# VectorE and ScalarE operations of a two-block decoder kernel wait for the last operation on their engine that they depend on, set call by call, instead of always for the one issued just ahead

## The reference

```python
for l in range(2):                      # first block
    h = rms_norm(x, norm_w[l]);  p = h @ w_in[l]
    qa, ka, va, za, ub, zb, qkv_c, b_c, a_c, zc = _split_cols(p)
    oa = sliding_window_sink_attention(rope(rms_norm(qa)), rope(rms_norm(ka)), va, sinks[l]) * silu(za)
    ob = conformer_conv_module(ub, ...) * silu(zb)      # 31 taps, layer norm, silu, a 512x512 map
    oc = rms_norm(gated_deltanet(qkv_c, b_c, a_c, ...)) * silu(zc)   # 4 taps, chunks of 128 tokens
    x = x + concatenate([oa, ob, oc]) @ w_out[l]
for i in range(2):                      # second block
    u, z = split(rmsnorm(x, g_pre[i]) @ w_in_2[i])
    y = pool_mixer(u) if i == 0 else rglru(causal_depthwise_conv_2(u))
    x = x + rmsnorm((y * silu(z)) @ w_out_2[i], g_post[i])
    gate = sigmoid(rmsnorm(x, g_ple_in[i]) @ w_ple_gate[i])
    x = x + rmsnorm((p[i] @ w_ple[i]) * gate, g_ple_out[i])
```

## Time and profile before

| | |
|---|---|
| median of 3 runs | 2496.28 us (2494.63 to 2497.04) |
| the profiled execution, its own time | 2496.72 us |
| its span in the profile | 2494.9 us |
| PE busy | 2429.7 us (97%), 14580 matmuls |
| PE loading weights | 2144.0 us (86%) |
| DVE busy | 1729.0 us (69%), 1895 instructions |
| ACT busy | 1281.8 us (51%), 1378 instructions |
| granted TensorE clock, mean | 0.993 |

### The profile page before, as it was taken

How to read it: one execution, slowest core, us unless ns; L and a number is a source line. 1 busy time by engine, 2 the same in 40 slices (tenths; PEclk the granted TensorE clock), 3 DMA queues, 4 the chain that set the end, 5 groups by cost and what they waited for, 6 DMA issues and landing times.

```text
span 2494.9 us, 34361 instructions
## 1 busy us (share of the span) xinstructions
PE 2429.7 (97%) x14580; PEld 2144.0 (86%) x14580; DVE 1729.0 (69%) x1895; ACT 1281.8 (51%) x1378; POOL 0.2 (0%) x4
## 2 busy tenths in 40 slices
PE   8999999999999999999999999999999999999997
PEld 8998888799988987888888888878888888888876
DVE  5789757666898567566657667666657757678774
ACT  5544345654452365644444434356656466566573
POOL 0000000000000000000000000000000000000000
PEclk9999999999999999999999999999999999999999
DMA  6553223455532234555555555555454545555553
GB/s 230 203 182 123 94 92 123 179 223 187 186 136 95 102 117 161 206 186 186 186 190 190 194 186 186 194 209 192 152 182 176 191 178 186 187 185 186 197 191 118
DMA packets 63978, 428.19 MB, mean 172 GB/s; under 512 B 7120, under 2 KB 7248, under 8 KB 14800
## 3 DMA queue, kind: packets, MB, share of 16 engines
q1 hardware_dynamic: 61280, 414.97, 46.2%
q10 hardware_dynamic: 2544, 11.01, 1.2%
HBM read 421.76 MB, written 4.19 MB: 171 GB/s over the span
## 4 chain that ended last, share of the span: by engine, by line
PE 71%; DVE 16%; ACT 7%; issue 5%; DMA 0%; DVEq 0%; ACTq 0%; SPq 0%
PE PS L419 69%; DVE WL L1643 4%; DVE Q L1608 3%; DVE Q L1612 3%; ACT Q L971 3%; DVE QA L1612 2%; ACT WH L985 2%; ACT QA L971 1%; PE PS L542 1%; DVE O L1608 1%; PE PS L647 1%; DVE QA L2207 0%; DVE QA L1608 0%; DVE X L1612 0%; DVE Q L1619 0%
## 5 line engine op out<-in xcount | busy, mean ns | idle before, releaser
L1643 DVE TENSOR_TENSOR WL<-W,WH 128x2048 fp32r<-128x2048 f32 (+2 forms) x392 | 859.6, 2202 | 456.1 <-ACT WH L985 455.4
L985 ACT ACTIVATE WH<-W 128x2048 fp32r<-128x2048 f32 (+2 forms) x392 | 716.0, 1839 | 459.5 <-PE PS L419 363.9
L419 PE MATMUL PS<-H,WH 128*128 128x256 f32 (+1 forms) x4864 | 947.5, 328 | 0.0
L419 PEld LDWEIGHTS PS<-H,WH 128*128 128x128 f32 x4864 | 714.0, 191 | 44.0
L419 PE MATMUL PS<-H,WL 128*128 128x256 f32 x3392 | 561.1, 285 | 12.3 <-DVE H L1612 9.1
L419 PEld LDWEIGHTS PS<-H,WL 128*128 128x128 f32 x3392 | 503.9, 191 | 59.0 <-issue 12.7
L419 PE MATMUL PS<-WH,H 128*128 128x512 f32 (+1 forms) x1408 | 366.6, 381 | 0.0
L419 PEld LDWEIGHTS PS<-WH,H 128*128 128x128 f32 x1408 | 259.0, 188 | 51.6
L419 PE MATMUL PS<-WH,YS 128*128 128x512 f32 x1024 | 273.8, 389 | 0.0
L419 PEld LDWEIGHTS PS<-WH,YS 128*128 128x128 f32 x1024 | 192.2, 188 | 40.1
L419 PE MATMUL PS<-WL,H 128*128 128x512 f32 (+1 forms) x704 | 217.0, 388 | 8.5 <-DVE H L1608 8.5
(11 more groups left out here) (140 smaller groups left out, 1572.7 us busy)
## 6 DMA issues: line engine op xcount, KB each, us to landing
W<-in_wall SPq DMA_DIRECT2D x374, 1024.0 KB, 4.8
W<-in_wall SPq DMA_DIRECT2D x24, 512.0 KB, 3.5
W<-in_wall SPq DMA_DIRECT2D x8, 536.0 KB, 3.5
X<-in_xT SPq DMA_DIRECT2D x8, 256.0 KB, 5.8
X<-in_x ACTq DMA_DIRECT2D x1, 2048.0 KB, 8.7
xsave<-X ACTq DMA_DIRECT2D x1, 2048.0 KB, 8.6
X<-xsave ACTq DMA_DIRECT2D x1, 2048.0 KB, 7.9
Q<-in_g_post ACTq DMA_DIRECT2D x8, 256.0 KB, 3.3
```

The costliest lines, as they stand in the source:

```text
L419: return e.matmul(o, l, r, start=start, stop=stop, skip_group_check=True)
L985: e.activation(WH[:, s % NSPL, 0:m], W[:, c % NRAW, 0:m], ACT.Copy).then_inc(*up("hi", c))
L1643: e.tensor_tensor(WL[:, c % NRAW, 0:m], W[:, c % NRAW, 0:m], WH[:, s % NSPL, 0:m].bitcast(F32), ALU.subtract).then_inc(*up("lo", c))
```

## The change

Both lists of the last signals are kept whole (`past`), and each call says with `lag` how many of the operations issued just ahead it need not wait for: lag 0 is the wait as before, lag 3 waits for the fourth last. By a count of the calls, 951 of DVE's 1503 such operations and 342 of ACT's 800 have a lag above 0. Two places are also written in another order. The core of the diff:

```diff
             def act(o, a, f, *sig, lag=0, **k):
-                if here["end"]:
-                    w.wait_ge(*here["end"])
+                if len(past) > lag:
+                    w.wait_ge(*past[-1 - lag])
                 sig = sig or ("step_a",)
                 e.activation(o, a, f, **k).then_inc(*up(*sig))
-                here["end"] = (K.sem[sig[0]], K.count[sig[0]])
+                past.append((K.sem[sig[0]], K.count[sig[0]]))
...
                     act(rn[:, 512 * k:512 * k + 512], sbank("dn", l, "ss", k), ACT.Ln, "dn_a", l, "ln", k,
-                        scale=1.0, bias=tb("eps"))
+                        scale=1.0, bias=tb("eps"), lag=min(k, 3))
...
-                    act(TT_[:, 512 * k:512 * k + 512], sbank("dn", l, "tu", k), ACT.Copy, "dn_a", l, "tu", k)
+                    act(TT_[:, 512 * k:512 * k + 512], sbank("dn", l, "tu", k), ACT.Copy, "dn_a", l, "tu", k,
+                        lag=k)
...
                             act(p3[:, h, c0:c1], s3[:, h, c0:c1], ACT.Exp, bias=sm[:, 56 + k:57 + k], scale=1.0,
-                                accum_out=sm[:, 80 + k:81 + k])
+                                accum_out=sm[:, 80 + k:81 + k], lag=min(2 * (h - 4 * q) + b_, 3))
...
-            def before():
-                if here["end"]:
-                    w.wait_ge(*here["end"])
+            def before(lag=0):
+                if len(past) > lag:
+                    w.wait_ge(*past[-1 - lag])
...
             def summed(dst, g):
                 w.wait_ge(*to("ev_a", g))
                 for b in range(2):
-                    tt(dst(b), dst(b), sums(g, b, 1), ALU.add)
-                    tt(dst(b), dst(b), rb(2), ALU.mult, *(("ev_v", g) if b else ()))
+                    tt(dst(b), dst(b), sums(g, b, 1), ALU.add, lag=b)
+                for b in range(2):
+                    tt(dst(b), dst(b), rb(2), ALU.mult, *(("ev_v", g) if b else ()), lag=1)
...
                         stt(CT[:, 4 * i + m, :], RAW[:, 4 * i + m, k:k + 256], wk, CT[:, 4 * i + m, :], ALU.mult,
-                            ALU.add, *end)
+                            ALU.add, *end, lag=n - 1 if k else m)
...
-                    tt(KB[:, cs], CK[:, cs], sbank("dn", l, "bt", k), ALU.mult, "dn_v", l, "kb", k)
+                    tt(KB[:, cs], CK[:, cs], sbank("dn", l, "bt", k), ALU.mult, "dn_v", l, "kb", k, lag=k)
...
                     tt(DS[:, cs], sbank("dn", l, "kk", k), DS[:, cs], ALU.mult, "dn_v", l, "kk", k)
-                    tt(quad(UU[:, cs]), quad(DS[:, cs]), tbl("lv2").unsqueeze(1).to_broadcast([128, 4, 128]), ALU.mult)
+                    w.wait_ge(*to("dn_p", l, "kq", k))
+                    tt(DI[:, cs], sbank("dn", l, "kq", k), DI[:, cs], ALU.mult, "dn_v", l, "kq", k, lag=1)
+                    tt(quad(UU[:, cs]), quad(DS[:, cs]), tbl("lv2").unsqueeze(1).to_broadcast([128, 4, 128]), ALU.mult,
+                       lag=1)
                     tt(quad(UU[:, cs]), quad(UU[:, cs]), ident.unsqueeze(1).to_broadcast([128, 4, 128]), ALU.add,
                        "dn_v", l, "uu", k)
-                    w.wait_ge(*to("dn_p", l, "kq", k))
-                    tt(DI[:, cs], sbank("dn", l, "kq", k), DI[:, cs], ALU.mult, "dn_v", l, "kq", k)
...
-                        stt(ACC[:, m, :], HB[:, m, k:k + 256], wk, ACC[:, m, :], ALU.mult, ALU.add, *end)
+                        stt(ACC[:, m, :], HB[:, m, k:k + 256], wk, ACC[:, m, :], ALU.mult, ALU.add, *end,
+                            lag=3 if k else m)
...
                         stt(s3[:, h, :], sbank("at", l, "s", h)[:, 0:384], 0.125, tbl("amask", 384), ALU.mult, ALU.add,
-                            "at_v", l, "s", h)
+                            "at_v", l, "s", h, lag=h % 4)
...
                         stt(X[:, t, cs], E[:, t, cs], SM[:, 12 + t:13 + t], X[:, t, cs], ALU.mult, ALU.add,
-                            *(("x_v", "end", l, i) if t else ()))
+                            *(("x_v", "end", l, i) if t else ()), lag=min(2 * i + t, 3))
```

More of the change, by code:

```diff
@@ L1021, in first_sums @@
                 for b in range(2):
-                    act(dst(b), sums(g, b, 0), ACT.Copy, *(("ev_a", g) if b else ()))
+                    act(dst(b), sums(g, b, 0), ACT.Copy, *(("ev_a", g) if b else ()), lag=b)
             def skip(n):
@@ L1113, in decays @@
                     act(heads(EG)[:, 2 * k:2 * k + 2, 1, :], quad(sbank("dn", l, "eg", k))[:, 1::2, :], ACT.Exp,
-                        "dn_a", l, "eg", k, scale=1.0, bias=0.0)
-                    act(DI[:, cs], DI[:, cs], ACT.Exp, "dn_a", l, "di", k, scale=1.0, bias=0.0)
+                        "dn_a", l, "eg", k, scale=1.0, bias=0.0, lag=2 if k else 0)
+                    act(DI[:, cs], DI[:, cs], ACT.Exp, "dn_a", l, "di", k, scale=1.0, bias=0.0, lag=1)
             def delta_net(l):
@@ L1212, in attention @@
                     w.wait_ge(*to("at_p", l, "qt", k))
-                    act(dst, sbank("at", l, "qt", k), ACT.Copy, "at_a", l, "qt", k)
+                    act(dst, sbank("at", l, "qt", k), ACT.Copy, "at_a", l, "qt", k, lag=min(k, 3))
                 yield from rest(3)
@@ L1540, in post @@
                     for t in range(2):
-                        act(E[:, t, 512 * i:512 * i + 512], bank(gi, t), ACT.Copy, *(("ev_a", gi) if t else ()))
+                        act(E[:, t, 512 * i:512 * i + 512], bank(gi, t), ACT.Copy, *(("ev_a", gi) if t else ()),
+                            lag=t)
                     if i:
@@ L1601, in after, with tt, stt, ts @@
                 s = up(*sig)
[L1602 removed]
+                past.append((s[0], K.count[sig[0]]))
                 return s
[L1605 to L1607 removed]
+            def tt(o, a, b, op, *sig, lag=0):
+                before(lag)
                 e.tensor_tensor(o, a, b, op).then_inc(*after(sig))
[L1610 to L1611 removed]
+            def stt(o, a, s, b, op0, op1, *sig, lag=0):
+                before(lag)
                 e.scalar_tensor_tensor(out=o, in0=a, scalar=s, in1=b, op0=op0, op1=op1).then_inc(*after(sig))
[L1614 to L1615 removed]
+            def ts(o, a, s1, s2, op0, op1, *sig, lag=0):
+                before(lag)
                 if s2 is None:
@@ L1728, in opening @@
                     ts(DIAG[:, t, :], ident, SM[:, 10 + t:11 + t], None, ALU.mult, None,
-                       *(("norm_v", n, "diag") if t else ()))
+                       *(("norm_v", n, "diag") if t else ()), lag=t)
                 for _ in range(1 if n == 4 else 2):
@@ L1955, in attention @@
                     copy(kr[:, t], q4[:, t, 12:16, :].unsqueeze(2).to_broadcast([128, 4, 2, 64]),
-                         *(("at_v", l, "kr") if t else ()))
+                         *(("at_v", l, "kr") if t else ()), lag=t)
                 yield from rest(7)
@@ L1983, in weights @@
                         tt(v, v, den[:, b_, hs].unsqueeze(2).to_broadcast([128, 4, c1 - c0]), ALU.mult,
-                           *(("at_v", l, "p", q) if b_ else ()))
+                           *(("at_v", l, "p", q) if b_ else ()), lag=b_)
                 def turned(q):
@@ L1989, in turned @@
                             w.wait_ge(*to("at_p", l, "turn", n))
-                            copy(AS[:, 512 * n:512 * n + 512], sbank("at", l, "turn", n), "at_v", l, "turn", n)
+                            copy(AS[:, 512 * n:512 * n + 512], sbank("at", l, "turn", n), "at_v", l, "turn", n,
+                                 lag=1 if n > 3 * q + 1 else 0)
                 scores(0)
@@ L2032, in block1 @@
                         ts(dst[:, :, t], bank(g, t)[:, 256 + 6 * k:262 + 6 * k], SM[:, 10 + t:11 + t], None, ALU.mult,
-                           None, *(("ev_v", g) if t and k else ()))
+                           None, *(("ev_v", g) if t and k else ()), lag=2 * t + k)
                 dc = begin(decays(l), first=True)
@@ L2177, in conv @@
                             stt(ucv[:, m, :], RAWL[:, m, k:k + 256], wk, ucv[:, m, :], ALU.mult, ALU.add,
-                                *(("uc_v", n) if k == 2 and m == 3 else ()))
+                                *(("uc_v", n) if k == 2 and m == 3 else ()), lag=3 if k else m)
                 def chain(n, gi):
```

137 lines of the change are left out of this document (69 added, 68 removed).

## The result

The changed kernel takes 2456.55 us (median of 4 runs, 2455.54 to 2457.49), the kernel before 2495.45 us (4 runs). The ratio is 0.9846, with a 95% interval from 0.9833 to 0.986: 38.9 us less. The profiled execution took 2455.95 us against 2496.72 us, so 40.8 us are to be explained, where the sum had 22.6.

A forecast was written before the change was run, and what follows sets the result against it. PE bounds the kernel (busy 2429.7 of 2494.9 us), so only its waits and the end can shrink: 16.8 from waits and end + 2.4 from closed stretches + 3.4 from the clock = 22.6 us, giving 2474 us, range 2465 to 2486 us.

The forecast's parts named there:

- The price of a wait: Each operation freed of waiting for the one in front saves 0.12 us on DVE, 0.13 on ACT; 0.19 with two waits.
- The first rival: A met wait is free on DVE, so only ACT gains: 2496 us; chance 0.09.
- the second (DVE held by PE): Rival: DVE gains, but time freed before its last wait for PE's chunk is lost again: 2483 us; chance 0.17.
- `tk`: PE's wait at L638 behind DVE, 3.9 us idle: 3.1 us won, 0.4 us a layer left.
- `kb`: PE's wait for DVE, 1.1 us, behind three operations that lose 0.19 us twice: closes, 1.1 us.
- Sums of squares: PE behind ACT's first `Ln`, two of four stretches of 9.7 us: 0.7 us a layer, 1.4 us.
- The clock: Six falls to 1.2 GHz behind idle PE stretches, 1.7 us each where PE is busy; two should go: 3.4 us.
- the first product of `w_out`: PE behind DVE's `H` (L1608), chain from DVE's masks, two of four stretches: 0.7 us a layer, 1.4 us.
- all five falls go: Rival of more than the sum: all first-block clock falls go (5.1 us more), 2 us stretches shrink: 2466 us, within the range.
- Stretches that close: Sixteen idle stretches of PE close, each worth 0.15 us more than its idle row: 2.4 us.
- `tv`: PE's wait at L638 behind ACT, whose evictions wait for a `Silu` behind DVE: closes, 2.8 us.
- The start: PE's first wait, 9.1 us, follows PE or a transfer: 0 gain.

The follow-up runs named there:

- the Square in thirds: Changed kernel with ACT's Square over the delta net's output, ahead of the sum over `oo`, in three parts, PE waiting part by part: 2452.15 us, ratio 0.983.

## Why the prediction was right in direction and wrong in size

**The price of a wait: right.** 0.12 us on DVE, 0.20 where there had been two waits, and 0.14 on ACT were measured, where 0.12, 0.19 and 0.13 were taken. The first rival (DVE gains nothing) is out: with DVE alone 28.3 us go. So is the second (DVE held by PE), which gave 2483 us: `tk` and `kb`, whose gain it dropped, closed.

**Sums of squares: wrong.** The step that failed is "the `scaled` eviction between them cannot come before PE's group ends: 0.7 us a layer". It counted only the taps behind that eviction. But DVE came to it at least 7.3 us late, so all that DVE had saved earlier arrived too. And a second chain was missed, ACT's taps in DVE's loop, 0.43 us a round in DVE's idle time. Either goes most of the way alone: the stretches close with DVE's taps alone (no row), and come down from 5.5 to 1.8 us with ACT's alone. 1.4 us were forecast, 6.0 measured. This alone would have given 2469 us; with the clock, below, it is 2464.

**The clock: mis-sized.** Five falls went instead of two, 8.5 us instead of 3.4. The one behind `tk` went as forecast. Of the three behind the sums of squares and the first product of `w_out` one was counted and all went: the sums of squares closed, and the stretch ahead of `w_out` is 1.88 us by matmul starts now, a length behind which no profile here has a fall. The one behind `oo` of layer 1 went by chance: the stretch is unchanged, and with lags on DVE alone both `oo` stretches had one. The case "all five falls go" stood among the rivals, with 2466 us; it was right in itself, and too small in the other terms.

**Stretches that close: mis-sized.** 0.15 us on top of the idle row was taken from one pair of rows, which itself differs by 0.24 us; 0.48 us was measured at the transposes of layer 1. `tv` and `tk` gave 8.5 instead of 6.5 us, also because the 0.4 us a layer that were to stay did not; attention gave 4.4 instead of 3.0, the second block 6.9 instead of 4.6.

**The start: not forecast, and chance.** PE's first wait was 9.1 us in the profile before and 8.0 after; the version with all lags 0 also had 8.0, and the others lay between 7.3 and 8.7. So 1.1 of the 2.3 us do not belong to the change. The other 1.2 us are the first rise of the clock, at 15.1 us before and at 11.4 us after: until then matmuls start 0.21 us apart that later start 0.12 us apart. It does not go with the lags either. With all lags 0 the rise came at 12.6 us and the 40th matmul at 15.1 us; with the Square in thirds and all lags in they came at 13.3 and 15.9 us.

**Two counts were wrong.** The eleven rows add up to 50.4 us, not 48.4. And of the six places of the first block that stay at about 2 us, four had no fall before, not five (there was one behind `oo` and one ahead of `w_out`, both in layer 1). Neither enters the sum.

**Right:** `kb`, the first product of `w_out`, the additions at the end, the two `oo` stretches that stay at 2.1 us, PE's waits at L638, L780 and WL that go.

The sum asked of each idle row how much nearer operations save. DVE and ACT had long been behind, so all of their savings counted, and the rows closed entirely. Only where PE itself starts the chain (`oo`, the last head, the first product of `w_out`) does the near chain alone decide, and there the sum was right.

## What to carry to other kernels

Ask of each idle stretch whether the engine that PE waits for is late by its own load or follows PE directly. In the first case everything counts that it has saved since it last waited for PE, and what the engines save that it waits for in turn (DVE's waits for ACT, in the loop above, were no slack), and closing one stretch moves the rest of the lateness to the next. Price a closed stretch by the starts of the matmuls around it, not by its idle row, and add the clock: one that is cut to below about 2 us never brought a fall here, one of 3 us always did.

## What the runs showed of the hardware that was not expected

- An operation that waits for the end of the one just in front of it on its engine costs 0.12 us on DVE, also between short ones (taps of 128 x 256 0.40 instead of 0.51 us apart) and 0.14 us on ACT.
- A PE stretch of 2.1 to 2.8 us in the first block was followed by a fall of the clock to 1.2 GHz in 24 of 47 cases, the same stretch in some runs and not in others. One of over 3 us always was (7 of 7), one of 1.2 to 2.0 us never (0 of 75). The page "TensorE: Matmul & The Clock Gate" of the Trainium skill, section "HAM oscillation — how this bites in real kernels", warns of longer idle times than most of these; here 16 of 34 stretches of 2.1 to 2.3 us were already followed by one.
- A fall of 3.4 us costs 1.7 us where PE is busy all through it, measured behind `oo` of layer 1, where nothing else changed.
